# RWKV chunk scan of a hybrid decoder: each chunk's matrices stored as 64 columns on its own half of the partitions

## The chip, the core and the metric

The kernel runs as one program on one core of a Trainium2 chip. The metric is device time in microseconds, from one launch to its end; lower is better. Engines are named as in the profile: PE is TensorE's matmul, PEld its weight load, DVE VectorE, ACT ScalarE, POOL GpSimd, SP SyncE (it issues the DMAs).

## What is computed

One step of a decoder of two layers, for a prompt of 512 tokens and eight decode tokens. Each layer runs three token mixers side by side (retention, differential attention, RWKV-7), merges them by gates, and ends in an MLP. The change touches one stage: the RWKV scan of the prompt, 8 heads of 64 channels, with a 64x64 state per head:

```python
def rwkv7_scan(r, w, k, v, a_vec, b_vec, s0):
    def step(S, inp):
        rt, wt, kt, vt, at, bt = inp
        sa = jnp.einsum('bhij,bhj->bhi', S, at)
        S = S * wt[:, :, None, :] + sa[..., None] * bt[:, :, None, :] + vt[..., None] * kt[:, :, None, :]
        return S, jnp.einsum('bhij,bhj->bhi', S, rt)
    xs = tuple(t.swapaxes(0, 1) for t in (r, w, k, v, a_vec, b_vec))
    S, y = lax.scan(step, s0, xs)
    return y.swapaxes(0, 1), S
...
        yc, s_rwkv = rwkv7_scan(r_h, decay.reshape(hs), k_h, v_h, -kk, kk * a_h, rwkv_s0[l].astype(f32))
```

## The kernel before

A loop on the chip runs the two layers, and a layer is a row of blocks; at the end of a block all engines meet. In a block each engine runs its own list of instructions in the order in which it is written, and waits on semaphores. The scan is one such block (lines 1902 to 2086), and nothing else runs beside it.

The 512 tokens are taken as four blocks of 128 (index `m`), each of two chunks of 64 (index `cc`; `n = 2 * m + cc` counts the chunks). Heads lie in pairs: `hp` is the pair (4), `g` the head in the pair (2), so that a head's 64 channels are one half of the partitions. The token-by-token recurrence of a chunk is replaced by matrices: `products` makes, for each head and block, the 128x128 matrix of inner products of two vectors (four kinds: `m_ba`, `m_br`, `m_ka`, `m_kr`), and DVE's `mask` multiplies it by a triangle mask that is zero outside the two 64x64 diagonal squares, since the two chunks of a block do not mix there. All later products use the 128x128 matrix, zeros and all.

A block `m` has three parts:

- **Lead-in.** DVE makes the start of the inverse (`m1`, then `xt`, lines 2017 and 2018), PE turns `xt` round, ACT copies it to `xm` (L2072), PE makes the `m_ka` products, DVE masks `m_br` and `m_ka` (L2008).
- **Five levels** (`lv` 1 to 5) double the solved part of the triangular system. In each, for `g` = 0 and 1: PE multiplies `m_ba` and `xm` (call it W, bank `pb[g]`), DVE masks the result into `m1` (L2029), PE multiplies `xt` and `m1` (X, `pb[2 + g]`, not at the last level) and `m1` and `xt` (Y, `pb[4 + g]`), and DVE adds X to `xm` (L2042) and Y to `xt` (L2044). In the first level PE also makes the `m_kr` products between W and X.
- **Two chunks**, one after the other. PE: state and `m_ka` times v give the right side, DVE copies it (L2049); `xt` times that gives `uu`, DVE copies it (L2051); then the update of the state in `pb[3]` (`btok` times `uu`, `ktok` times v, as 128x128 of which two squares are wanted), then the output in `pb[2]` (`r_` times the state, `m_br`, `m_kr`). DVE masks the update (L2058), adds it to the state `stb` (L2060) and scales it (L2061), and then the next chunk can start. The `m_ba` and `m_br` products of the next block stand between these on PE.

All operands are fp32. A matmul of this stage shows as two PE records, each with a weight load before it: eight matmuls W of one level are 16 records.

Of the kernel before, what the change touches and what calls it, by code (L numbers as in the profile page):

```python
# [23 lines left out]
P = 128  # L24
# [14 lines left out]
HP = HC // 2  # L39
# [16 lines left out]
for _n, _w in (("ident", P), ("ones", P), ("blk", P), ("inner", HA * P), ("cross", HA * P), ("keep", 2 * P),  # L56
               ("level", 6 * P), ("cosq", 320), ("sinq", 320), ("cosk", 320), ("sink", 320), ("tail", HA),
               ("chunk", HA), ("gamma", HA), ("scan", T), ("c0", HB * DEC), ("c1", HB * DEC), ("selb", DEC),
               ("pair", 2), ("laminit", 2 * DEPTH), ("vmix", DEPTH), ("fold", 9), ("toe", TOE), ("past", NPG * P)):
    COL[_n] = (_c, _w)  # L60
    _c += _w
# [22 lines left out]
def shape_constants():  # L84
# [21 lines left out]
    same = (i[:, None] // CH) == (i[None, :] // CH)  # L106
    before = same & (i[:, None] < i[None, :])
    upto = same & (i[:, None] <= i[None, :])
    put("keep", np.stack([before, upto], 1))
    lv = []  # L110
    for k in range(6):
        m = 1 << k
        lv.append((i[:, None] // (2 * m) == i[None, :] // (2 * m)) & (i[:, None] % (2 * m) >= m)
                  & (i[None, :] % (2 * m) < m))
    lv[0] = lv[0].T
# [88 lines left out]
def build(nc, a, consts, outs):  # L204
# [7 lines left out]
    with ExitStack() as ctx:  # L212
# [257 lines left out]
        with nc.Fori(0, DEPTH) as l:  # L470
# [1422 lines left out]
            m_ba, m_br, m_ka, m_kr = (at(ring[0], n * 1024, 2, HP, P) for n in range(4))  # L1893
            xt = at(arena, 6240, 2, HP, P)
            xm = at(y_raw, 8 * T, 2, HP, P)
            m1 = at(y_raw, 8 * T + 1024, 2, HP, P)
            rhs1 = ring[1][:, 3200:3712]
            uu = arena[:, 7264:7776]
            keep = C("keep", 2, P)
            level = C("level", 6, P)  # L1900
            states_stored = c["stored"].next(256)
            with nc.Block() as block:
                @block.tensor
                def _(pe):
                    def products(left, right, m, bank, g):

                        gs, tok = slice(g * 64, (g + 1) * 64), slice(m * P, (m + 1) * P)
                        for hp in range(HP):
                            t = mm(pb[bank + g][:, hp * P:(hp + 1) * P], left[gs, hp, tok], right[gs, hp, tok])
# [6 lines left out]
                    for m in range(MT):  # L1916

                        for g in range(2):
                            pe.wait_ge(y_added, 12 * m + g + 1)
                            for hp in range(HP):  # L1920
                                t = tr(pb[g][:, hp * P:(hp + 1) * P], xt[:, g, hp, :])
                            t.then_inc(x_made, 1)

                        if m:
                            pe.wait_ge(state_done, 2 * m)
                            pe.wait_ge(out_copied, 2 * m)
                        products(k_, z2, m, 2, 0)
                        products(k_, z2, m, 2, 1).then_inc(ka_made, 1)
                        pe.wait_ge(ba_masked, m + 1)
                        for lv in range(1, 6):  # L1930
                            for g in range(2):
# [4 lines left out]
                                for hp in range(HP):  # L1936
                                    t = mm(pb[g][:, hp * P:(hp + 1) * P], m_ba[:, g, hp, :], xm[:, g, hp, :])
                                t.then_inc(w_made, 1)
                            if lv == 1:
# [4 lines left out]

                                pe.wait_ge(ka_masked, m + 1)
                            for g in range(2):
# [3 lines left out]
                                for hp in range(HP):  # L1950
                                    hs = slice(hp * P, (hp + 1) * P)
                                    if lv < 5:
                                        mm(pb[2 + g][:, hs], xt[:, g, hp, :], m1[:, g, hp, :])
                                    t = mm(pb[4 + g][:, hs], m1[:, g, hp, :], xt[:, g, hp, :])
                                t.then_inc(y_made, 1)
                        pe.wait_ge(kr_masked, m + 1)
                        pe.wait_ge(y_added, 12 * (m + 1))
                        for cc in range(2):
                            n = 2 * m + cc
                            r = slice(cc * 64, (cc + 1) * 64)  # L1960
                            tk = slice(m * P + cc * 64, m * P + (cc + 1) * 64)
                            hsl = [slice(h * 64, (h + 1) * 64) for h in range(HC)]

                            if n:
                                pe.wait_ge(state_done, n)
                            for hp in range(HP):
                                mm(pb[0][r, hp * P:(hp + 1) * P], z2[:, hp, tk], stb[:, hp, :], start=(hp == 0), stop=False)
                            for h in range(HC):
                                t = mm(pb[0][r, hsl[h]], m_ka[r, h % 2, h // 2, r], vtok[r, m, hsl[h]], start=False)
# [4 lines left out]
                            for h in range(HC):  # L1974
                                t = mm(pb[1][r, hsl[h]], xt[r, h % 2, h // 2, r], rhs1[r, hsl[h]])
                            t.then_inc(u_made, 1)
                            if m + 1 < MT:
                                products(z1, (z2, r_)[cc], m + 1, 4 + 2 * cc, 1).then_inc((ba_made, br_made)[cc], 1)
                            pe.wait_ge(u_copied, n + 1)
                            for hp in range(HP):  # L1980
                                hs = slice(hp * P, (hp + 1) * P)
# [3 lines left out]
                            if cc:  # L1985
# [473 lines left out]
```

## Time and profile before

| | us |
|---|---|
| median of 3 runs | 3525.27 (3522.18 to 3531.48) |
| profiled execution, its own time | 3527.91 |
| span of that execution, first to last instruction | 3526.0 |
| the scan, layer 0 and layer 1 | 246.87 and 246.74 |
| one block of 128 tokens in it (`m` = 1, layer 0) | 57.71 |

The span is what the trace shows; 1.9 us of the time lie around it. The scan's two stretches are 493.6 us, 14% of the span. Over the whole span PE is busy 83%, DVE 47%, ACT 22% and POOL 5%. Since each block of the program ends with a meeting of all engines and nothing runs beside the scan, a microsecond that the scan loses or gains is one of the whole.

### The profile page before, as it was taken

The numbers are of one execution on the slowest core, as the hardware profiler recorded it, in microseconds if no ns is written. First come the engines' busy times: TensorE is split into PE (matmuls) and PEld (weight loads), VectorE is DVE, ScalarE is ACT, GpSimd is POOL, SyncE is SP. The second block draws the span as 40 slices with busy tenths as digits, with TensorE's granted clock in tenths as the row PEclk, the third lists the DMA queues.
The fourth block names the chain that finished last, engine by engine and source line by source line (L and its number), as shares of the span: only waits on it lengthen the run. The fifth ranks groups of instructions, "written<-read, shape, count | busy, mean of one in ns | idle before, by whom it ended". The sixth has DMA issues, their size and how long they took to land. (4 is left out here: it accounts for less than half of the span.)

```text
span 3526.0 us, 47932 instructions
## 1 busy us (share of the span) xinstructions
PE 2925.7 (83%) x20182; PEld 2603.1 (74%) x20182; DVE 1643.4 (47%) x2052; ACT 780.9 (22%) x1106; POOL 162.1 (5%) x100
## 2 busy tenths in 40 slices
PE   2698888894899787999948879898849997979898
PEld 1477775793788487999936767578748885979898
DVE  3415345428555564324422441743475546553343
ACT  0221224223100032323302111322320002232331
POOL 0002110200000000000000210121000000000000
PEclk9898998995599688999969889899858986989999
DMA  2413345611000151222241230663100003412221
GB/s 104 179 36 94 101 139 179 206 31 34 13 1 1 42 182 67 77 92 72 72 178 54 57 120 24 226 193 122 47 6 7 1 1 110 157 48 96 72 96 49
DMA packets 212993, 298.61 MB, mean 85 GB/s; under 512 B 27901, under 2 KB 96969, under 8 KB 211492
## 3 DMA queue, kind: packets, MB, share of 16 engines
q1 hardware_dynamic: 212772, 295.47, 25.3%
q8 instruction: 162, 2.65, 0.3%
q14 instruction: 59, 0.48, 0.0%
HBM read 260.30 MB, written 35.14 MB: 84 GB/s over the span
## 5 line engine op out<-in xcount | busy, mean ns | idle before, releaser
L361 PE MATMUL pb<-h_high,f_high 128*128 128x260 f32 x2048 | 417.5, 285 | 62.5 <-ACTq L2319 41.2
L361 PE MATMUL pb<-h_high,f_low 128*128 128x260 f32 x2048 | 416.1, 285 | 0.0
L361 PE MATMUL pb<-h_low,f_high 128*128 128x260 f32 x2048 | 415.1, 284 | 0.0
L361 PEld LDWEIGHTS pb<-h_high,f_high 128*128 128x128 f32 x2048 | 320.2, 191 | 63.7 <-issue 41.9
L511 DVE TENSOR_TENSOR w_low<-ring,w_high 128x2048 fp32r<-128x2048 f32 x64 | 146.7, 2293 | 422.4 <-ACT w_high L503 420.9
L361 PEld LDWEIGHTS pb<-h_low,f_high 128*128 128x128 f32 x2048 | 319.6, 190 | 0.0
L361 PEld LDWEIGHTS pb<-h_high,f_low 128*128 128x128 f32 x2048 | 318.1, 191 | 0.0
L511 DVE TENSOR_TENSOR f_low<-ring,f_high 128x2048 fp32r<-128x2048 f32 x64 | 146.7, 2293 | 349.9 <-ACT h_high L505 204.6
L361 PE MATMUL pb<-w_high,h_high 128*128 128x512 f32 x560 | 225.2, 402 | 52.7 <-ACTq L819 40.8
L738 POOL TENSOR_TENSOR g_low<-yT,g_high 128x512 fp32r<-128x512 f32 x96 | 161.9, 1691 | 2248.3 <-ACT g_high L734 2248.3
L364 PE MATMUL pb<-cst,arena 128*128 128x128 f32 (+5 forms) x566 | 117.0, 351 | 173.5 <-PEq L540 77.8
L361 PE MATMUL pb<-arena 64*128 64x128 f32 (+4 forms) x1520 | 229.7, 349 | 29.6 <-DVE arena L922 9.4
L364 PEld LDWEIGHTS pb<-cst,arena 128*128 128x128 f32 (+5 forms) x566 | 78.1, 170 | 210.3 <-issue 129.1
L361 PEld LDWEIGHTS pb<-arena 64*128 64x128 f32 (+3 forms) x1520 | 184.7, 205 | 63.8 <-issue 38.0
L361 PE MATMUL pb<-w_high,h_low 128*128 128x512 f32 x560 | 224.5, 401 | 0.0
L361 PE MATMUL pb<-w_low,h_high 128*128 128x512 f32 x560 | 224.4, 401 | 0.0
L361 PE MATMUL pb<-h_high,g_high 128*128 128x260 f32 x768 | 169.0, 303 | 45.1 <-POOL g_low L738 24.2
L503 ACT ACTIVATE f_high<-ring 128x2048 fp32r<-128x2048 f32 x64 | 122.6, 1915 | 370.1 <-PE pb L361 342.1
L503 ACT ACTIVATE w_high<-ring 128x2048 fp32r<-128x2048 f32 x64 | 122.1, 1914 | 356.0 <-PE pb L361 219.9
L361 PEld LDWEIGHTS pb<-h_high,g_high 128*128 128x128 f32 x768 | 127.3, 203 | 63.6 <-POOL g_low L738 40.7
L361 PEld LDWEIGHTS pb<-w_high,h_high 128*128 128x128 f32 x560 | 107.5, 192 | 79.3 <-issue 41.6
L361 PE MATMUL pb<-h_low,g_high 128*128 128x260 f32 x768 | 162.2, 294 | 0.0
(309 smaller groups left out, 5287.3 us busy)
## 6 DMA issues: line engine op xcount, KB each, us to landing
ring<-in_w_ff_dram SPq DMA_DIRECT2D x32, 2048.0 KB, 8.5
ring<-in_w_ada_dram SPq DMA_DIRECT2D x20, 2048.0 KB, 8.4
ring<-in_w_in_dram SPq DMA_DIRECT2D x20, 2048.0 KB, 8.7
yT<-in_w_in_dram SPq DMA_DIRECT2D x96, 256.0 KB, 3.6
gate_spill_dram<-yT SPq DMA_DIRECT2D x48, 260.0 KB, 4.2
arena<-gate_spill_dram SPq DMA_DIRECT2D x12, 1040.0 KB, 5.2
arena<-in_w_ada_dram SPq DMA_DIRECT2D x4, 2048.0 KB, 20.4
arena<-in_cache_k_diff_dram SPq DMA_DIRECT2D x32, 256.0 KB, 3.5
```

The source lines that it names most:

```text
L361: return PE.matmul(out, lhsT, rhs, start=start, stop=stop, skip_group_check=True)
L364: return PE.transpose(out, in_, ident[0:in_.shape[0], 0:in_.shape[0]])
L503: t = S.activation(ws[n % 2][0], ring[slot][:, u * 2048:(u + 1) * 2048], ACT.Copy)
L511: t = V.tensor_tensor(ws[n % 2][1], ring[slot][:, u * 2048:(u + 1) * 2048], ws[n % 2][0].bitcast(F32), sub)
L738: G.tensor_tensor(g_split[j % 2][1], g_raw[j % 2], g_split[j % 2][0].bitcast(F32), sub).then_inc(gate_ready, 1)
```

## The change

The two 64x64 squares of a block's matrix are stored below each other instead of on the diagonal of a 128x128 one: chunk 0 on partitions 0 to 63, chunk 1 on partitions 64 to 127, each with 64 columns. So `m_ba` and its like, `xt`, `xm` and `m1` are half as wide, and so are the masks. A product of 128x128 becomes two of 64x64, one for each chunk, from rows and columns 0 to 63 of PE and from rows and columns 64 to 127 in turn (`head_products`). `products` makes the two squares of a head only. The turn of `xt` is no transpose any more but a product with the identity. The state's update is made per head as a 64x64 square on the head's half of the partitions; DVE keeps the state in `stc` in that form, and writes it into the two squares of `stb`, whose other squares stay zero, for the products that read it. In a chunk, products that don't need the state are written ahead of the waits. X and Y share a bank.

```diff
-            m_ba, m_br, m_ka, m_kr = (at(ring[0], n * 1024, 2, HP, P) for n in range(4))
-            xt = at(arena, 6240, 2, HP, P)
+            m_ba, m_br, m_ka, m_kr = (at(ring[0], n * 512, 2, HP, CH) for n in range(4))
+            xt = at(arena, 6240, 2, HP, CH)
...
+            stc, stn = at(ring[0], 2048, HP, DC), at(ring[0], 2304, HP, DC)
+            lower = [slice(cc * CH, (cc + 1) * CH) for cc in range(2)]
...
                         for hp in range(HP):
-                            t = mm(pb[bank + g][:, hp * P:(hp + 1) * P], left[gs, hp, tok], right[gs, hp, tok])
+                            for cc in range(2):
+                                tok = slice(m * P + cc * CH, m * P + (cc + 1) * CH)
+                                t = mm(at(pb[bank + g], 0, HP, CH)[lower[cc], hp], left[gs, hp, tok], right[gs, hp, tok])
                         return t
+                    def head_products(out, left, right, g):
+                        for hp in range(HP):
+                            for cc in range(2):
+                                t = mm(out[lower[cc], hp], left[lower[cc], g, hp], right[lower[cc], g, hp])
                         return t
...
-                                t = tr(pb[g][:, hp * P:(hp + 1) * P], xt[:, g, hp, :])
+                                for cc in range(2):
+                                    t = mm(at(pb[g], 0, HP, CH)[lower[cc], hp], xt[lower[cc], g, hp], ident[lower[cc], lower[cc]])
...
+                            for h, hp, g, hs, gs in heads:
+                                mm(pb[2][r, hs], m_ka[r, g, hp], vtok[r, m, hs], start=(h == 0), stop=False)
                             if n:
                                 pe.wait_ge(state_done, n)
...
+                            upd = at(pb[0], 0, HP, DC)
+                            for h, hp, g, hs, gs in heads:
+                                mm(upd[gs, hp], ktok[r, m, hs], vtok[r, m, hs], start=(hp == 0), stop=False)
...
-                                mm(pb[3][:, hs], btok[r, m, hs], uu[r, hs], stop=False)
-                                t = mm(pb[3][:, hs], ktok[r, m, hs], vtok[r, m, hs], start=False)
+                            for h, hp, g, hs, gs in heads:
+                                t = mm(upd[gs, hp], btok[r, m, hs], uu[r, hs], start=False, stop=True)
                             t.then_inc(update_made, 1)
...
-                            dv(V.tensor_tensor(upd, at(pb[3], 0, HP, P), bc(blk, [P, HP, P], 1), mult))
-                            v.wait_ge(state_read, n + 1)
-                            dv(V.tensor_tensor(stb, stb, upd, add))
-                            V.tensor_tensor(stb, stb, bc(dend[:, :, n], [P, HP, P], 2), mult).then_inc(state_done, 1)
-                            v.wait_ge(state_done, n + 1)
+                            dv(V.tensor_tensor(stn, stc, at(pb[0], 0, HP, DC), add))
+                            for g in range(2):
+                                gs = lower[g]
+                                t = V.tensor_tensor(stb[gs, :, gs], stn[gs], bc(dend[gs, :, n], [DC, HP, DC], 2), mult)
+                            t.then_inc(state_done, 1)
+                            dv(V.tensor_tensor(stc, stn, bc(dend[:, :, n], [P, HP, DC], 2), mult))
```

How the instructions stand, at the three places that the prediction speaks of. A row is a line of the kernel, an operation, what it writes and reads, the size of what it writes (partitions x elements), how many alike follow, and the semaphores that it waits for.

PE, level 2 of a block, the two W and the first X and Y, before (`ring` is `m_ba`, `arena` is `xt`, and `yT` is `xm` or `m1`):

```order
L361 MATMUL pb<-yT,ring 128x128 [waits x_added]
L361 MATMUL pb<-yT,ring 128x128 x3
L361 MATMUL pb<-yT,ring 128x128 [waits x_added]
L361 MATMUL pb<-yT,ring 128x128 x3
L361 MATMUL pb<-yT,arena 128x128 [waits y_added,w_masked]
L361 MATMUL pb<-arena,yT 128x128
```

And in the changed kernel, whose line numbers are one lower here:

```order
L360 MATMUL pb<-yT,ring 64x64 [waits x_added]
L360 MATMUL pb<-yT,ring 64x64 x7
L360 MATMUL pb<-yT,ring 64x64 [waits x_added]
L360 MATMUL pb<-yT,ring 64x64 x7
L360 MATMUL pb<-yT,arena 64x64 [waits y_added,w_masked]
L360 MATMUL pb<-yT,arena 64x64 x7
L360 MATMUL pb<-arena,yT 64x64 x8
```

The order and the waits are the same; each matmul has become two of a quarter of the size, X comes as eight and then Y as eight, where they alternated.

PE, the first chunk of block 0, before (64x128 from `arena` alone are the products with the state, `arena,ring` those with `m_ka`, `m_br` and `m_kr`, `ring,arena` is `xt` times the right side, and 128x128 are `products` and the update):

```order
L361 MATMUL pb<-arena 64x128 [waits y_added,kr_masked]
L361 MATMUL pb<-arena 64x128 x3
L361 MATMUL pb<-arena,ring 64x64 x8
L361 MATMUL pb<-arena 128x128 x4
L361 MATMUL pb<-ring,arena 64x64 [waits rhs_copied]
L361 MATMUL pb<-ring,arena 64x64 x7
L361 MATMUL pb<-arena 128x128 x4
L361 MATMUL pb<-arena 128x128 [waits u_copied]
L361 MATMUL pb<-arena 128x128 x7
L361 MATMUL pb<-arena 64x128 x4
L361 MATMUL pb<-arena,ring 64x64 x16
```

The same chunk in the changed kernel:

```order
L360 MATMUL pb<-arena,ring 64x64 [waits y_added,kr_masked,ka_masked]
L360 MATMUL pb<-arena,ring 64x64 x7
L360 MATMUL pb<-arena 64x128 x4
L360 MATMUL pb<-arena 64x64 x16
L360 MATMUL pb<-ring,arena 64x64 [waits rhs_copied]
L360 MATMUL pb<-ring,arena 64x64 x7
L360 MATMUL pb<-arena 64x64 x8
L360 MATMUL pb<-arena,ring 64x64 x8
L360 MATMUL pb<-arena 64x128 x4
L360 MATMUL pb<-arena 64x64 [waits u_copied]
L360 MATMUL pb<-arena 64x64 x7
L360 MATMUL pb<-arena,ring 64x64 x8
```

The `m_ka` products stand ahead of the state's, half of the update (`ktok` times v) ahead of the first copy, and `m_kr` and `r_` times the state ahead of the second; only half of the update and `m_br` stand behind it.

DVE, the same chunk, before (L2049 and L2051 are the two copies, L2008 masks `m_ba` of the next block, L2058 to L2061 are the state):

```order
L2049 COPY ring<-pb 64x512 [waits rhs_made]
L2051 COPY arena<-pb 64x512 [waits u_made]
L2008 TENSOR_TENSOR ring<-pb,cst 128x512 [waits ba_made]
L2008 TENSOR_TENSOR ring<-pb,cst 128x512
L2058 TENSOR_TENSOR yT<-pb,cst 128x512 [waits update_made]
L2060 TENSOR_TENSOR arena<-arena,yT 128x512 [waits state_read,dve_done]
L2061 TENSOR_TENSOR arena<-arena,small 128x512 [waits dve_done]
```

And in the changed kernel:

```order
L2060 COPY ring<-pb 64x512 [waits rhs_made]
L2062 COPY arena<-pb 64x512 [waits u_made]
L2018 TENSOR_TENSOR ring<-pb,cst 128x256 [waits ba_made]
L2018 TENSOR_TENSOR ring<-pb,cst 128x256
L2069 TENSOR_TENSOR ring<-ring,pb 128x256 [waits update_made,state_read]
L2072 TENSOR_TENSOR arena<-ring,small 64x4x64 [waits dve_done]
L2072 TENSOR_TENSOR arena<-ring,small 64x4x64
L2074 TENSOR_TENSOR ring<-ring,small 128x256
```

The two copies keep their size, the masks are half as wide, and the three steps on the state have become four of half the width, of which three come before the next chunk may read it.

## Rows read from the trace of the kernel before

**Rows 1.** Table by stretch (from:to us, length, busy per engine (records), clock, DMA): the scan, both layers

```profile
943.53:1190.40 246.87, 232.67 (x1956) 215.33 (x1956) 132.12 (x201) 9.51 (x16) 0.00 (x0) 0.88 0.00 1
2669.60:2916.34 246.74, 230.14 (x1958) 212.95 (x1956) 132.15 (x201) 10.27 (x18) 0.00 (x0) 0.89 0.00 1
```

**Rows 2.** Same table: block 1's lead-in, levels, chunks, whole; then block 3, layer 0

```profile
1005.57:1019.39 13.82, 12.12 (x82) 10.95 (x81) 7.84 (x12) 1.79 (x3) 0.00 (x0) 0.75 0.01 1
1019.39:1043.35 23.96, 23.08 (x192) 21.81 (x190) 16.82 (x26) 0.00 (x0) 0.00 (x0) 1.00 0.00 1
1043.35:1063.28 19.93, 19.82 (x220) 18.35 (x220) 8.19 (x13) 0.59 (x1) 0.00 (x0) 1.00 0.01 2
1005.57:1063.28 57.71, 55.02 (x492) 51.11 (x490) 32.85 (x50) 2.38 (x4) 0.00 (x0) 0.94 0.00 1
1121.07:1190.40 69.33, 62.65 (x468) 57.35 (x466) 32.26 (x49) 2.97 (x5) 0.00 (x0) 0.77 0.00 1
```

**Rows 3.** Timeline (start us, length us, instructions xcount, idle before): end of a level, block 0

```profile
968.82 0.39 PE L361 MATMUL pb<-arena,yT 128*128 128x128 f32 x2
969.04 2.10 PE L361 MATMUL pb<-yT,ring 128*128 128x128 f32 x16
969.24 0.69 DVE L2042 TENSOR_TENSOR yT<-yT,pb 128x512 f32<-128x512 f32 x1 [0.50 <-PE pb L361]
969.85 0.68 DVE L2044 TENSOR_TENSOR arena<-arena,pb 128x512 f32<-128x512 f32 x1
970.45 1.43 DVE L2029 TENSOR_TENSOR yT<-pb,cst 128x512 f32<-128x512 f32 x2
971.18 0.30 PEld L361 LDWEIGHTS pb<-yT,arena 128*128 128x128 f32 x2 [0.23 <-DVE yT L2029]
```

**Rows 4.** Timeline: first chunk of block 0 on PE, and DVE's first copy

```profile
985.75 1.06 PE L361 MATMUL pb<-arena 128*64 128x128 f32 x8 [0.87 <-DVE arena L2044]
986.74 1.14 PE L361 MATMUL pb<-arena,ring 64*64 64x64 f32 x16
987.81 1.16 PE L361 MATMUL pb<-arena 64*128 64x128 f32 x8
987.91 0.68 DVE L2049 COPY ring<-pb 64x512 f32<-64x512 f32 x1 [2.32 <-PE pb L361]
989.96 3.91 PE L361 MATMUL pb<-arena 64*128 64x128 f32 x32
993.81 2.08 PE L361 MATMUL pb<-arena,ring 64*64 64x64 f32 x32
995.81 0.43 PE L361 MATMUL pb<-arena 128*64 128x128 f32 x2
```

**Rows 5.** Groups by form (busy us, mean ns, idle): 32-column products; two-column products

```profile
L361 PE MATMUL pb<-arena,xT 128*32 128x512 f32 x32 | 3.6, 595 | 0.6 <-DVEq L1380 0.6
...
L361 PE MATMUL pb<-cst,yT 128*8 128x2 f32 x8 | 0.3, 165 | 0.0
```

**Rows 6.** Timeline: attention scores of one unit; the scan's first products, layer 1

```profile
555.35 1.13 PE L361 MATMUL pb<-arena 64*128 64x512 f32 x4
...
2671.02 2.79 PE L361 MATMUL pb<-arena 64*128 64x128 f32 x32 [1.03 <-PEq L1796]
```

**Rows 7.** Timeline: DVE on 256 elements a partition, in the stage before

```profile
933.80 0.42 DVE L1876 TENSOR_TENSOR ring<-pb,arena 128x256 f32<-128x256 f32 x1 [1.56 <-PE pb L361]
934.14 0.41 DVE L1877 TENSOR_TENSOR ring<-ring,pb 128x256 f32<-128x256 f32 x1
934.58 0.42 DVE L1878 TENSOR_TENSOR ring<-ring,pb 128x256 f32<-128x256 f32 x1
```

**Rows 8.** Table by stretch: second chunk of block 3; start of block 1; 8-row products

```profile
1169.11:1185.79 16.68, 15.04 (x98) 13.66 (x98) 3.46 (x5) 0.59 (x1) 0.00 (x0) 0.50 0.00 0
1008.30:1015.00 6.70, 6.62 (x32) 6.07 (x33) 2.96 (x6) 0.63 (x2) 0.00 (x0) 0.50 0.01 2
...
919.50:933.30 13.80, 13.80 (x62) 12.46 (x61) 8.54 (x22) 1.19 (x2) 0.00 (x0) 0.50 0.11 25
```

More of the change, by code:

```diff
@@ L55 @@
 COL = {}
[L56 to L57 removed]
+for _n, _w in (("ident", P), ("ones", P), ("blk", P), ("inner", HA * P), ("cross", HA * P), ("keep", 2 * CH),
+               ("level", 6 * CH), ("eye", CH), ("cosq", 320), ("sinq", 320), ("cosk", 320), ("sink", 320), ("tail", HA),
                ("chunk", HA), ("gamma", HA), ("scan", T), ("c0", HB * DEC), ("c1", HB * DEC), ("selb", DEC),
@@ L105, in shape_constants @@
     put("gamma", np.broadcast_to(np.exp(log_g)[None], (P, HA)))
[L106 to L109, printed above, removed]
+    row, col = (i % CH)[:, None], np.arange(CH)[None, :]
+    put("keep", np.stack([row < col, row <= col], 1))
+    put("eye", row == col)
     lv = []
@@ L1949, in _ @@
                                     pe.wait_ge(y_added, 12 * m + 2 * (lv - 1) + g + 1)
[L1950 to L1955, printed above, removed]
+                                xy = at(pb[2 + g], 0, 2, HP, CH)
+                                if lv < 5:
+                                    head_products(xy[:, 0], xt, m1, g)
+                                head_products(xy[:, 1], m1, xt, g).then_inc(y_made, 1)
+                        pe.wait_ge(ka_masked, m + 1)
                         pe.wait_ge(kr_masked, m + 1)
@@ L1978, in _ @@
                                 products(z1, (z2, r_)[cc], m + 1, 4 + 2 * cc, 1).then_inc((ba_made, br_made)[cc], 1)
+                            if n:
+                                pe.wait_ge(out_copied, n)
+                            for h, hp, g, hs, gs in heads:
+                                mm(pb[3][r, hs], m_kr[r, g, hp], vtok[r, m, hs], start=(h == 0), stop=False)
+                            for hp in range(HP):
+                                t = mm(pb[3][r, hp * P:(hp + 1) * P], r_[:, hp, tk], stb[:, hp], start=False, stop=False)
@@ L1984, in _ @@
                             t.then_inc(update_made, 1)
-                            if cc:
-                                pe.wait_ge(out_copied, n)
-                            for hp in range(HP):
-                                t = mm(pb[2][r, hp * P:(hp + 1) * P], r_[:, hp, tk], stb[:, hp, :], start=(hp == 0), stop=False)
-                            t.then_inc(state_read, 1)
-                            for h in range(HC):
-                                mm(pb[2][r, hsl[h]], m_br[r, h % 2, h // 2, r], uu[r, hsl[h]], start=False, stop=False)
-                                t = mm(pb[2][r, hsl[h]], m_kr[r, h % 2, h // 2, r], vtok[r, m, hsl[h]], start=False)
+                            for h, hp, g, hs, gs in heads:
+                                t = mm(pb[3][r, hs], m_br[r, g, hp], uu[r, hs], start=False, stop=True)
@@ L1993, in _ @@
                             t.then_inc(out_made, 1)
-                    pe.wait_ge(state_done, 2 * MT)
+                    pe.wait_ge(dve_for_pe, c["pe_from_dve"].next())
                     for hp in range(HP):
-                        t = tr(pb[0][:, hp * P:(hp + 1) * P], stb[:, hp, :])
+                        for g in range(2):
+                            t = mm(at(pb[0], 0, HP, DC)[lower[g], hp], stc[lower[g], hp], ident[lower[g], lower[g]])
                     t.then_inc(pe_for_dve, 1)
@@ L2001, in _ @@
                     dv = c["dve"]
+                    dv(V.memset(stc, 0.0))
                     v.wait_ge(stored, states_stored)
@@ L2024, in _ @@
                         v.wait_ge(ka_made, m + 1)
-                        mask(m_ka, 0, 2).then_inc(ka_masked, 1)
+                        mask(m_ka, 0, 4).then_inc(ka_masked, 1)
                         for lv in range(1, 6):
```

77 lines of the change are left out of this document (36 added, 41 removed).

## The prediction, written before the changed kernel ran

> **What bounds the kernel now.** First the table by stretch: the scan takes 246.87 and 246.74 us [rows 1], together 493.6 of 3526; in it PE is busy 232.67 of 246.87 us, DVE 132.12, and no DMA runs. Only this stage changes, so the question is what each part of one block of 128 tokens waits for. Block 1 takes 57.71 us: 13.82 of lead-in, 23.96 of levels (first add to last), 19.93 of chunks [rows 2]. Four such blocks, a short opening and an end make the layer; block 3 is longer, 69.33 us, because the clock falls to 0.50 (1.2 GHz) in its chunks.
>
> A level repeats every 5.81 us. The timeline shows the loop [rows 3]: the last X and Y record starts 0.11 after 968.82, DVE adds at 969.24 and 969.85 and masks at 970.45, and at 971.18 PE begins the next X and Y. With 32 records of X and Y at 0.11 us (two from 968.82 to 969.04) the loop is 3.52 + 0.31 (from the last record to DVE's start) + 0.61 + 0.60 + 0.73 = 5.77. So it is PE's X and Y plus DVE's two adds and a mask; W (16 x 0.11 = 1.76) lies beside the DVE part. A chunk is PE alone: 985.75 to 995.81, 10.06 us, group after group without a wait worth naming [rows 4].
>
> **The prices that the change needs.** A record of 64x64 after another in the same quarter of PE: 32 take 2.08 us [rows 4], less 0.22 for the last one's length, so 0.060. The change alternates two quarters. What two cost side by side no row shows at 64 columns. The lower bound is full overlap, 0.030 a record; the upper is none, 0.060. I take 0.030, for three rows. Four strips of 32 columns in turn: 32 records of 512 columns in 3.6 us, where one such record alone streams 4 x 0.11 = 0.44, so 14 us in sequence; four ran at once [rows 5]. Two halves of the rows in turn, the attention scores: 4 records in 1.13 us instead of 4 x 0.44 + 0.15 = 1.9 [rows 6]. And in this very stage, at full clock, the 32 opening products of 64 rows, which change the half only every eight records, take 2.79 us instead of 32 x 0.11 + 0.28 = 3.8 [rows 6]. In all three a matmul also stands as two records in sequence before the other strip's come, as it will here. Issue is no limit either: eight two-column records take 0.3 us with 0.165 for the last [rows 5], so at most 0.027 apart. Here the Trainium skill speaks against the change: "TensorE: Matmul & The Clock Gate", section "Wait — 56ns, not 53.3ns?", says that with hardware decode off the sequencer spends about 62 ns on every matmul, which binds once the array's work is shorter. By it nothing would overlap, and the time would be rival 1's; the 0.027 says that this chip doesn't run so.
>
> DVE: 0.42 for 256 elements a partition, 0.34 to the next start where it doesn't depend on the last, 0.44 to 0.46 where it does [rows 7], against 0.61 to 0.73 for 512 [rows 3]. From PE's last record to DVE's start 0.25 (a 64x64 record's 0.22 and 0.03), from DVE's end to PE 0.05.
>
> **Part by part, for one block at full clock.**
>
> *Levels.* X and Y become 64 records: 64 x 0.030 = 1.92. Loop: 1.92 + 0.25 + 0.34 + 0.34 + 0.42 + 0.05 = 3.32. PE's own sum, 96 x 0.030 = 2.88, is below it, so PE no longer binds; DVE's adds and mask do half. From the first add to the end of the last: four loops 13.28, the last Y 2 x 0.48, 0.25 and 0.42, less the first X and Y half and its way to DVE (0.96 + 0.25): 13.7, against 23.96.
>
> *Lead-in.* DVE's first half of `xt` is there after 0.88, its second after 1.68 (was 2.8). From there PE runs the turn of the second half (0.48), `m_ka` (32 records, 0.96), W (0.96), `m_kr` (0.96), and the first X and Y (0.96); with 0.25 to DVE, 6.3 at full clock. ACT's copies (under 0.6 each, [rows 2]) and DVE's masks lie beside these. At 1.2 GHz a pair takes 2 x 0.0534 (half the clock of 64 x 2 columns at 2.4), and 160 records are 8.5; 0.93 + 8.5 + 0.3 = 9.8. Before, the clock stood at 0.50 for 6.7 us in this place of every block [rows 8], after a stretch in which PE waits for DVE; the changed kernel has such a stretch too, only shorter, so I take the middle, 8.1, for blocks 1 to 3, and 9.8 for block 0, which follows a stage at half clock. Before: 13.82.
>
> *Chunks.* On PE, per chunk: two products with the state, each 0.99 with the change of tile size behind it (985.75 to 986.74, [rows 4]); four groups of 16 in one quarter (`m_ka`, `xt`, `m_kr`, `m_br`), 4 x 0.96 = 3.84, and about 0.1 for each of two changes of tile size; and four groups of 16 that alternate between column halves (two of `products`, the two halves of the update), 4 x 0.48 = 1.92. Sum 7.9, against 10.06: what falls away is the update's and the products' empty half. The waits fit beneath: after the state's product PE has 0.96 of work for the 1.04 of the first copy (0.31 + 0.68 + 0.05), more than 2 for the second, and `m_br` and the next `m_ka` (1.92) cover DVE's state steps (0.22 + 0.46 + 0.34 + 0.42 + 0.05 = 1.5). The two copies keep 64x512 and 0.68. In the second chunk the block ends at the update: 7.9 less `m_br` (0.96), 0.25, and 1.65 of DVE until the next lead-in. 7.9 + 6.95 + 0.25 + 1.65 = 16.75, against 19.93.
>
> *Sum.* A block: 8.1 + 13.7 + 16.75 = 38.55, against 57.71. The layer: opening 2.8 (4.5 before, from the first product to the first DVE step); block 0 40.25; blocks 1 and 2 77.1; block 3, whose chunks have no `products` (7.5 and 6.75) and end with the state's steps, a turn by 16 records and a copy (1.6 + 1.2): 38.85. Together 159.0, against 246.8. That the clock holds in block 3's chunks is part of this: they are shorter by the waits and the half-empty update. Twice 87.8 is 175.6. Profiled time 3527.9 - 175.6 = 3352.3; the median lies 2.6 below that execution, so **3350**. Clearing `stc` and the smaller constants cost nothing: DVE waits for the opening products then.
>
> **Rivals.**
>
> 1. *The quarters don't overlap, the clock holds.* A level is bound by PE: 96 x 0.060 = 5.76, no gain on 5.81; levels 23.5, lead-in 10.8, chunks 9.86 + 8.9 + 1.9 = 20.7: a block saves 2.7, block 3 up to 14, the opening 1. Twice about 20 gives 3490. For it: nothing at 64 columns shows an overlap. Against: the three rows above.
>
> 2. *They don't overlap, and the clock doesn't rise.* This is the one that ends slower. PE would stream 64 rows at a time. The rows show that a busy PE isn't enough: with 8-row products it was busy 13.80 of 13.80 us and stayed at 0.50; at the start of block 1, with 64-row products first, 6.62 of 6.70 at 0.50 [rows 8]; and block 3's second chunk took 16.68 instead of 10. At 0.107 a record: lead-in 18.3, levels 4 x 10.3 + 0.4 = 41.5, chunks 17.6 + 15.9 + 1.9 = 35.4, so 95 a block. The layer is longer by 140, the time 3805. It decides from the opening on: block 0 of each layer begins at 0.50, and in this case nothing before the first product with the state would lift it.
>
> 3. *They overlap, but the clock stays at 1.2 GHz throughout.* Level max(96 x 0.0534, 64 x 0.0534 + 1.46) = 5.1; levels 20.9, lead-in 9.8, chunks 28.6: 59.3, 1.6 worse than before in three blocks, but block 3, slow already, gains 10.7 and the opening 1.7. Twice 7.6 gives 3512. For it: each layer's scan opens near the half clock, and in block 3's chunks, which have no `products`, it fell to 0.50. Against: in block 1 it rose once W, X and Y ran, and held 1.00 through the levels and the chunks, whose records are mostly of 64 rows [rows 2].
>
> **How the numbers follow.** Forecast 0.80, rival 1 0.05, rival 3 0.08, rival 2 0.07. About 0.3% (11 us) is what a measurement of this kernel can tell from no change. Forecast and rival 1 are faster, and rival 3 (3512, a gain of 13) in half of its cases: faster 0.89, same 0.04, slower 0.07. Within the forecast: all lead-ins at 6.3 take 11 off, and a level loop without the 0.05s another 10, so 3325; an overlap half good, 0.045 a record, costs 0.96 a level and 8.9 a block, 71 in all, so 3421. The range goes on to rival 1, to 3500: that leaves out rivals 2 and 3 and the forecast's tails, nearly 2 in 10.
>
> **What would show it.** The scan near 159 us a layer. The level loop near 3.3 us, with PE idle between Y and the next X and Y until DVE's mask is done; a row of 32 records of X or Y under 1.2 us. If it is 1.9 and the loop 5.8, the quarters don't overlap. Clock 1.00 through levels and chunks, block 3 no longer than the others; a row of 0.50 across the levels is rival 2 or 3. Chunks 7.9 apart; if more, a wait for `rhs_copied` or `state_done` that I put beneath PE's work. The forecast is wrong if two records in different quarters start 0.06 apart, or if the clock falls where only one quarter streams.

## The result and the profile after

The changed kernel takes 3339.35 us in the median of four runs (3326.39 to 3341.77), the kernel before 3523.72 (3517.59 to 3531.48): a ratio of 0.9478 with a 95% interval of 0.9441 to 0.9515, faster. The forecast was 3350 with a range of 3325 to 3500. The profiled execution is the fastest of the four, 3326.39, with a span of 3324.5; the one before has 3526.0.

The scan's two layers, against 246.87 and 246.74 in [rows 1] and a forecast of 159.0 (table by stretch: from:to us, length, busy time per engine with records, granted clock, DMA share, GB/s):

```profile
941.78:1092.07 150.29, 137.50 (x3344) 127.19 (x3344) 85.86 (x210) 7.79 (x16) 0.00 (x0) 0.97 0.01 3
2563.23:2713.44 150.21, 137.52 (x3344) 127.20 (x3344) 85.85 (x210) 7.79 (x16) 0.00 (x0) 0.97 0.01 3
```

That is 493.6 - 300.5 = 193.1 us less, out of 201.5 between the two spans. The other 8.4 us aren't the change's: the span less both layers is 3032.4 before and 3024.0 after, and over the twelve kernels profiled in this study it lies between 3019.0 and 3035.0 without order. These stages are the same in all of them. So a single execution carries some 8 us either way that the scan has no part in, the two medians of the changed kernel (here and in e0) lie 7 us apart, and small effects are read below from the scan's length, not from the medians.

The parts of block 1, which answer to [rows 2]: lead-in, levels, chunks, whole; then block 0's lead-in, and block 3 of layer 0.

```profile
979.54:986.61 7.07, 6.03 (x171) 5.88 (x173) 4.64 (x13) 0.77 (x2) 0.00 (x0) 0.76 0.01 2
986.61:1000.19 13.58, 12.88 (x381) 11.71 (x375) 9.89 (x26) 0.00 (x0) 0.00 (x0) 1.00 0.01 4
1000.19:1016.79 16.60, 15.47 (x288) 14.32 (x288) 6.79 (x15) 1.18 (x2) 0.00 (x0) 1.00 0.01 3
979.54:1016.79 37.25, 34.38 (x832) 31.91 (x832) 21.32 (x53) 1.95 (x4) 0.00 (x0) 0.95 0.01 3
...
943.70:949.37 5.67, 4.62 (x170) 4.49 (x172) 4.45 (x13) 0.77 (x2) 0.00 (x0) 1.00 0.01 4
...
1054.16:1092.07 37.91, 34.08 (x784) 31.30 (x784) 21.07 (x51) 1.95 (x4) 0.00 (x0) 0.95 0.01 3
```

In block 0's lead-in the 32 records of `m_ka` begin at 945.83 and W behind them at 946.49, those of `m_kr` at 947.42 and X behind them at 948.06 (timeline: start us, length us, engine, line, output<-inputs, shapes, count):

```profile
945.83 0.27 PE L360 MATMUL pb<-arena 64*64 64x64 f32 x1
...
946.49 0.27 PE L360 MATMUL pb<-yT,ring 64*64 64x64 f32 x1
...
947.42 0.27 PE L360 MATMUL pb<-arena 64*64 64x64 f32 x2
...
948.06 0.27 PE L360 MATMUL pb<-yT,arena 64*64 64x64 f32 x1
```

Block 3, 69.33 us before, is no longer an exception: its clock is 0.95. PE's busy time in the scan fell from 232.67 to 137.50 us although its records rose from 1956 to 3344.

A level on DVE, against [rows 3] (timeline: start us, length us, engine, line, output<-inputs, shapes, count, idle before and its releaser). L2053 adds X, L2055 adds Y, once for each half of the heads; L2039 masks W; the PE row is the start of the next X.

```profile
993.15 0.42 DVE L2053 TENSOR_TENSOR yT<-yT,pb 128x256 f32<-128x256 f32 x1 [0.71 <-PE pb L360]
993.49 0.41 DVE L2055 TENSOR_TENSOR arena<-arena,pb 128x256 f32<-128x256 f32 x1
994.08 0.42 DVE L2053 TENSOR_TENSOR yT<-yT,pb 128x256 f32<-128x256 f32 x1 [0.18 <-PE pb L360]
994.42 0.41 DVE L2055 TENSOR_TENSOR arena<-arena,pb 128x256 f32<-128x256 f32 x1
994.75 0.96 DVE L2039 TENSOR_TENSOR yT<-pb,cst 128x256 f32<-128x256 f32 x2
995.22 0.68 PE L360 MATMUL pb<-yT,arena 64*64 64x64 f32 x16
996.42 0.42 DVE L2053 TENSOR_TENSOR yT<-yT,pb 128x256 f32<-128x256 f32 x1 [0.71 <-PE pb L360]
```

The loop, from one L2053 to the next of the same half, is 3.27 us; it was 5.81. The second half's add still waits for PE (0.18), then come an add, an add and a mask (0.42 each, 0.34 from start to start), and 0.05 after the first mask's end PE starts the next X, as in the forecast's sum. On PE, groups of 16 records of one product (timeline):

```profile
955.23 0.63 PE L360 MATMUL pb<-arena,yT 64*64 64x64 f32 x16
955.69 0.63 PE L360 MATMUL pb<-yT,arena 64*64 64x64 f32 x16
```

0.63 from the first start to the last end, less 0.22 for the last record's own length, is 0.41 for seven more pairs: 0.058 a pair, where one quarter alone took 0.060 a record [rows 4]. Two quarters (of 64 rows by 64 columns of PE each) do run side by side.

### The profile page after: what moved, and what is told of

Its sections match the earlier page's. It is cut to its first block and busy times, and to the rows that moved or that the text cites. A ratio compares the mean times of both kernels' runs of the same rounds, so it can differ in the third digit from the quotient of the medians.

```text
span 3324.5 us, 53480 instructions
## 1 busy us (share of the span) xinstructions
PE 2726.0 (82%) x22958; PEld 2423.9 (73%) x22958; DVE 1552.3 (47%) x2070; ACT 777.6 (23%) x1106; POOL 162.9 (5%) x100
## 5 line engine op out<-in xcount | busy, mean ns | idle before, releaser
L363 PE MATMUL pb<-cst,arena 128*128 128x128 f32 (+5 forms) x494 | 95.0, 334 | 158.3 <-PEq L539 78.0
L363 PEld LDWEIGHTS pb<-cst,arena 128*128 128x128 f32 (+5 forms) x494 | 64.8, 163 | 188.9 <-issue 124.2
L360 PE MATMUL pb<-arena 64*64 64x64 f32 (+6 forms) x2288 | 176.7, 279 | 22.3 <-DVE arena L921 9.4
L360 PEld LDWEIGHTS pb<-arena 64*64 64x64 f32 (+4 forms) x2288 | 135.4, 158 | 52.1 <-issue 29.7
```

The costliest lines, as they stand in the source:

```text
L360: return PE.matmul(out, lhsT, rhs, start=start, stop=stop, skip_group_check=True)
L363: return PE.transpose(out, in_, ident[0:in_.shape[0], 0:in_.shape[0]])
```

## Experiments

Each kernel, the profiled spans of both scan layers added up, and the rest of its span. The first four stand against a kernel before of 3522.98 (3517.65 to 3538.44), the next four against 3526.78 (3524.35 to 3533.07), the last two against 3526.67 (3519.79 to 3537.07).

| kernel | median us (range) | ratio to before, 95% | both scan layers | rest of span |
|---|---|---|---|---|
| before | 3523.72 | 1 | 493.6 | 3032.4 |
| changed | 3339.35 (3326.39 to 3341.77) | 0.9478, 0.9441 to 0.9515 | 300.5 | 3024.0 |
| e1 levels, one quarter at a time | 3386.66 (3380.32 to 3393.01) | 0.9608, 0.9521 to 0.9695 | 351.0 | 3027.4 |
| e2 columns in blocks | 3349.16 (3346.57 to 3351.76) | 0.9502, 0.9424 to 0.9579 | 321.6 | 3023.1 |
| e3 DVE doubled | 3378.47 (3370.39 to 3386.54) | 0.9585, 0.9491 to 0.9678 | 349.5 | 3019.0 |
| e4 chunk order of before | 3385.30 (3383.67 to 3386.93) | 0.9604, 0.9527 to 0.9681 | 353.7 | 3028.1 |
| e0 changed kernel again | 3332.27 (3325.34 to 3335.48) | 0.9442, 0.9425 to 0.9458 | 300.7 | 3029.8 |
| e5 levels staggered | 3327.76 (3313.91 to 3333.96) | 0.9443, 0.9427 to 0.9458 | 287.5 | 3024.6 |
| e6 four quarters | 3329.92 (3323.80 to 3332.97) | 0.9435, 0.9420 to 0.9451 | 293.4 | 3035.0 |
| e7 stagger, four quarters, v for both chunks | 3304.51 (3299.14 to 3308.55) | 0.9370, 0.9355 to 0.9386 | 274.4 | 3022.8 |
| e8 early opening | 3308.40 (3304.82 to 3311.64) | 0.9375, 0.9352 to 0.9399 | 279.5 | 3030.3 |
| e9 all, and early opening | 3287.88 (3283.22 to 3290.53) | 0.9317, 0.9293 to 0.9342 | 257.6 | 3029.7 |

**Is it the turn of the quarters? (e1)** In the levels the two chunks' products stand one behind the other instead of in turn; nothing else changes.

```diff
-for hp in range(HP):
-    for cc in range(2):
+for cc in range(2):
+    for hp in range(HP):
         t = mm(out[lower[cc], hp], left[lower[cc], g, hp], right[lower[cc], g, hp])
...
+for cc in range(2):    # X (8 records), then Y (8), of one chunk
```

> The changed kernel with the order inside the level products turned: all of chunk 0 and then all of chunk 1, so that 8 records (W) or 16 (X with Y) in a row use the same quarter of PE. Same work, same waits. Theory A (the gain of the levels is that two quarters of PE stream side by side): most of the overlap goes. With none at all a level is 96 x 0.058 = 5.6 us; where PE looks a few records ahead at each of 8 changes of quarter, as the opening products of before did (1.0 us saved at 3 changes), 4.4 to 4.9. So the loop lies between 4.4 and 5.6 us instead of 3.27, the levels at 18 to 23 instead of 13.6 us a block, and the time at 3390 to 3450 us if the clock holds, up to 3700 if PE falls to 1.2 GHz in the levels. Theory B (the gain is that DVE's masks and adds are half as wide): the loop stays at 3.3 us and the time at 3340.

The loop becomes 4.58 us and the layers 175.4 and 175.6: 50 us for an order alone, so theory B falls. One loop, and PE in it (table by stretch, then timeline):

```profile
955.80:960.38 4.58, 4.58 (x100) 4.50 (x98) 2.26 (x6) 0.00 (x0) 0.00 (x0) 1.00 0.02 4
```

```profile
958.97 0.45 PE L360 MATMUL pb<-arena,yT 64*64 64x64 f32 x5
959.21 0.27 PE L360 MATMUL pb<-yT,arena 64*64 64x64 f32 x1
959.26 0.22 PE L360 MATMUL pb<-arena,yT 64*64 64x64 f32 x1
959.31 0.22 PE L360 MATMUL pb<-yT,arena 64*64 64x64 f32 x1
959.32 0.22 PE L360 MATMUL pb<-arena,yT 64*64 64x64 f32 x1
```

PE is busy throughout: it is the bound again, as in the kernel before. But 4.58 is nearer to the lower end of A's 4.4 to 5.6, and the time just under A's range. The second fence shows why: records go alone, 0.058 apart, until some three are left in their quarter; then the other quarter's first products start between them (959.21, 959.26, 959.31, 959.32). So the overlap doesn't need neighbours in strict turn; it reaches a few records ahead, and where 16 stand in one quarter most of it is lost.

**The same for the other products (e2).** The products that prepare a block (`products`) and both halves of the update run eight records in one quarter before the other's eight; the levels and the turn of `xt` stay as they were.

```diff
-for hp in range(HP):
-    for cc in range(2):        # in products
+for cc in range(2):
+    for hp in range(HP):
...
-for h, hp, g, hs, gs in heads:  # the update, both times
+for h, hp, g, hs, gs in heads[::2] + heads[1::2]:
```

> The changed kernel with the same turn in the products of two vectors and in the two halves of the state's update (same half of the rows, column halves no longer in turn but 8 records of one and 8 of the other). Theory A: these groups of 16 records take 0.75 to 0.95 us instead of 0.48; lead-in 7.1 to about 8.5 us, chunks from 16.6 to 19 or 20 us a block, time about 3365 to 3385 us. Theory C (two column halves of the same rows don't stream side by side anyway, and the chunks gained only by their new order): no change, 3340 us.

The layers take 163.6 and 158.0, 21 us more in all (layer 0 is the longer because its opening and lead-ins met more of a granted clock of 0.50), and the median rises by 10 to 17: between the two theories. The medians alone couldn't tell, since the intervals of the ratios overlap (0.9424 to 0.9579, and 0.9441 to 0.9515). A chunk goes from 7.50 and 7.73 to 8.27 and 8.20, a lead-in at full clock from 5.67 to 6.79; the level loop stays at 3.27. With blocks of eight, the few records ahead are a larger share (timeline, the change from one quarter to the other inside the chunk):

```profile
972.23 0.27 PE L360 MATMUL pb<-ring,arena 64*64 64x64 f32 x1
972.28 0.22 PE L360 MATMUL pb<-arena 64*64 64x64 f32 x1
972.34 0.22 PE L360 MATMUL pb<-ring,arena 64*64 64x64 f32 x1
972.34 0.22 PE L360 MATMUL pb<-arena 64*64 64x64 f32 x1
972.39 0.22 PE L360 MATMUL pb<-ring,arena 64*64 64x64 f32 x1
972.40 0.22 PE L360 MATMUL pb<-arena 64*64 64x64 f32 x1
```

A's price was that of no overlap; the right one is that of an overlap only where quarters meet.

**Does DVE's chain close the loop? (e3)** Before every mask and add of the levels stands one more operation of 256 elements into a tile that nobody reads.

```diff
+V.tensor_tensor(pad[2 + g], bc(level[:, lv], ...), bc(eye, ...), add)
 V.tensor_tensor(xm[:, g], xm[:, g], xy[:, 0], add).then_inc(x_added, 1)
```

> The changed kernel with a second DVE instruction of 128x256, on constants and into a spare tile, ahead of each mask and add of the levels: DVE's part of the levels has its old length again, PE's is untouched. Theory A with the loop of the prediction (X and Y, then two adds and a mask of DVE): 1.87 + 0.25 + 5 x 0.34 + 0.42 + 0.05 = 4.3 us a level instead of 3.27, the levels near 18 us a block, time about 3375 us. If PE alone sets the loop (theory D): 3.3 us and 3340 us.

A loop and the DVE rows in it:

```profile
956.28:960.96 4.68, 3.37 (x104) 3.04 (x101) 4.10 (x13) 0.00 (x0) 0.00 (x0) 1.00 0.02 4
```

```profile
955.94 0.43 DVE L2055 TENSOR_TENSOR ring<-cst 128x256 f32<-128x256 f32 x1 [0.58 <-PE pb L360]
956.28 0.41 DVE L2056 TENSOR_TENSOR yT<-yT,pb 128x256 f32<-128x256 f32 x1
956.62 0.42 DVE L2058 TENSOR_TENSOR ring<-cst 128x256 f32<-128x256 f32 x1
```

The loop is 4.68, 1.41 longer, and 32 loops make 45 of the scan's 49 us: with the doubled steps DVE sets the loop, and theory D's 3.3 falls. That it did so before the doubling isn't shown by this run, since twelve steps of 0.335 are 4.0 us, more than 3.27 whatever bound the loop; e5 below shows it. The size was A's 4.3 plus 0.38, and the first row tells where that comes from: DVE now starts on the first half of X and Y (0.58 of idle there) and has no wait left for the second. Its ten steps up to the first mask, 9 x 0.335 + 0.42, the first half's 0.93 and 0.27, and 0.05 to PE make 4.68. In the changed kernel both halves of X and Y and only three steps stood in this path.

**What the new order in the chunk is worth (e4).** The quarters stay; the products with `vtok`, the update's first part and `r_` times the state go back to where the kernel before has them, behind the waits. The order, in short:

```diff
-m_ka x vtok; wait state_done; z2 x stb; update from ktok
+wait state_done; z2 x stb; m_ka x vtok
...
-m_kr x vtok; r_ x stb; wait u_copied; update from btok; m_br x uu
+wait u_copied; update from ktok, btok; r_ x stb; m_br x uu, m_kr x vtok
```

> The changed kernel with the chunk's products in the order of the kernel before (state before m_ka, the whole update and then r_ times the state, m_br and m_kr behind the second copy), still as quarters. Theory A (a chunk is bound by PE's records, and got shorter because the update and the products lost their empty halves): PE now waits about 0.55 us for each of the two copies, and the chunks go from 16.6 us to about 19 a block; time near 3358 us. Theory E (the new order is what made the chunks shorter): they go back to 19.9 us or more a block, time 3366 us or more.

The layers take 177.4 and 176.4, 53 us more. That is on E's side and beyond A's 3358, but the rows don't show waits of that size. First e4's layer 0, its first chunk of block 0, the second up to the fall of the clock and the rest of it, and most of block 1's second chunk, behind another fall; then the changed kernel's two chunks:

```profile
946.99:1124.36 177.37, 164.25 (x3344) 151.80 (x3344) 85.88 (x210) 7.79 (x16) 0.00 (x0) 0.80 0.01 2
...
969.26:976.85 7.59, 6.65 (x121) 6.00 (x122) 2.45 (x5) 0.00 (x0) 0.00 (x0) 1.00 0.01 2
976.85:983.81 6.96, 6.08 (x117) 5.57 (x117) 2.66 (x5) 0.59 (x1) 0.00 (x0) 1.00 0.01 2
983.81:987.18 3.37, 3.37 (x35) 2.92 (x31) 0.42 (x1) 0.00 (x0) 0.00 (x0) 0.50 0.00 0
...
1019.00:1033.36 14.36, 14.00 (x142) 12.79 (x140) 2.67 (x6) 0.59 (x1) 0.00 (x0) 0.50 0.01 1
```

```profile
1000.19:1007.69 7.50, 7.36 (x142) 6.91 (x143) 2.45 (x5) 0.00 (x0) 0.00 (x0) 1.00 0.01 2
1007.69:1015.42 7.73, 7.73 (x148) 7.16 (x147) 3.08 (x6) 0.59 (x1) 0.00 (x0) 1.00 0.01 4
```

At full clock the old order costs 0.09 us in the first chunk (7.59 against 7.50). The second takes 10.33, of which 3.37 at 0.50; with half of those off it would be some 8.6 (an estimate), against 7.73. That is about 1 us a block, 8 us of the 53. What the old order does besides is to leave PE idle, 0.94 us of 7.59 and 0.88 of 6.96 instead of 0.14 and none, and behind that the granted clock falls to 0.50, where a chunk needs over 14 us. The scan's mean clock is 0.80, not 0.97. So most of the order's worth is the clock it keeps, not the waits that it hides. That the idle time is what brings the clock down here is read from this sequence alone; no run kept the old order without the idle. The kernel before agrees: in its blocks 0 to 2 the chunks leave PE idle for at most 0.15 us and hold 1.00, in block 3 for over 1.6 us each, and there the clock falls.

**The changed kernel again, and what repeats (e0).** An unchanged copy.

> The changed kernel once more, beside the three edits below, to see what repeats. Theory A (quarters overlap in pairs): a scan layer is again 150 us, a level loop 3.27 us, two chunks 16.6 us, and the time is 3326 to 3342. What differs between executions is where the attention stages and the copies ahead of the scan meet a granted clock of 0.5; theory F (the scan itself scatters): the layer differs from 150.3 by more than 2 us.

Layers of 150.36 and 150.35, loops of 3.27, chunks of 7.50 and 7.72: theory A, the scan repeats to 0.1 us, with three falls of the clock in every layer both times. The single lead-ins don't repeat: block 0's is 7.14 here and 5.67 above, block 3's 5.67 here and 7.17 above. Here are two of them, at either clock:

```profile
1055.53:1061.20 5.67, 4.62 (x170) 4.48 (x172) 4.45 (x12) 0.77 (x2) 0.00 (x0) 1.00 0.01 3
1018.16:1025.35 7.19, 6.14 (x171) 6.00 (x173) 4.64 (x12) 0.77 (x2) 0.00 (x0) 0.76 0.01 3
```

It is the same work, 1.5 us apart by whether the clock fell.

**What bounds a level now (e5).** The halves are staggered, so that DVE's steps on one half lie beside PE's products of the other; Y gets banks of its own. In short:

```diff
-for g: W(lv, g);  for g: X(lv, g), Y(lv, g)
+X(lv, 0), Y(lv, 0), X(lv, 1), W(lv + 1, 0), Y(lv, 1), W(lv + 1, 1)
```

> The same products as the changed kernel, but the two halves of heads staggered: X of half 0, Y of half 0, X of half 1, W of half 0 for the next level, Y of half 1, W of half 1; Y goes to banks of its own so that a half waits for its X alone. Theory A: what is left of a level is TensorE work of 6 x 0.47 = 2.8 us plus a wait at the turn of 0.45 us; the stagger covers that wait, a loop is 2.8 to 2.9 us instead of 3.27, 32 loops save some 13 us: 3325 against 3340. Theory G: VectorE's six operations of 0.42 to 0.44 us and their hand-overs set the loop now, it stays at 3.05 to 3.3 and the time falls by 0 to 7 us.

Two loops of e5, and two of the changed kernel:

```profile
956.42:962.02 5.60, 5.60 (x200) 5.60 (x198) 5.08 (x12) 0.00 (x0) 0.00 (x0) 1.00 0.01 3
```

```profile
952.64:959.18 6.54, 6.42 (x199) 5.91 (x196) 4.52 (x13) 0.00 (x0) 0.00 (x0) 1.00 0.02 5
```

A loop takes 2.80, with PE busy for all of it: theory A. So 0.47 of the changed kernel's 3.27 were PE's wait for DVE, and the scan is 13.2 us shorter. The median shows only 4.5 of that against e0; the profiled pair gives 18.4, of which 5.2 lie outside the scan.

**Four quarters (e6).** In `products` both halves of the heads come in turn too. In a chunk this also puts all of `products` ahead of the wait for the first copy, where half of it stood behind.

```diff
 for hp in range(HP):
+    for g_ in range(2):
         for cc in range(2):
```

> The products of 64 columns that open and prepare a block (z1 x z2, z1 x r, k x z2, k x r) take both halves of heads and both chunks in turn, so that four neighbours in the stream lie on all four quarters of the array; written to the same places. Theory H: four quarters run side by side as two do, a pair of records 7 ns apart becomes a group of four, 32 products take 0.47 instead of 0.93 us; four such groups per block lie on the path in part: 10 to 15 us less, 3325 to 3330. Theory I: no more than two products are in flight, whatever their quarters: no change, 3340.

A layer's first 64 records (32 matmuls), in e6 and in the changed kernel (timeline):

```profile
947.85 1.16 PE L360 MATMUL pb<-arena 64*64 64x64 f32 x64 [1.03 <-PEq L1795]
```

```profile
941.78 1.56 PE L360 MATMUL pb<-arena 64*64 64x64 f32 x64 [1.23 <-PEq L1795]
```

1.16 less 0.22 for the last record's length, over 16 groups of four, is 0.059 a group: four run side by side as two do, theory H. The changed kernel's pairs would need 32 x 0.058 + 0.22 = 2.08 there; it takes 1.56, since at its change of half the next records reach ahead. The scan gains 7.1 us, not 10 to 15; the medians can't tell that from nothing (ratio 0.9435 against e0's 0.9442).

**Both, and the products with v for both chunks at once (e7).**

```diff
+if cc == 0:
     for h, hp, g, hs, gs in heads:
-        mm(pb[2][r, hs], m_ka[r, g, hp], vtok[r, m, hs], ...)
+        for rr in lower:
+            mm(pb[2][rr, hs], m_ka[rr, g, hp], vtok[rr, m, hs], ...)
...                              # m_kr into pb[3] likewise
```

> The stagger of the levels and the four quarters together, and in the chunks the products of the masked matrices with v for both chunks side by side (written once per block, 32 products of 64 columns in pairs, in place of 2 x 16 alone). Theory A with H: the stagger saves 13 us, the four quarters 10 to 15, and pairing the products with v 16 x 0.030 us twice per block, about 1 us per block or 8 us if they lie on the path: some 3300 to 3305. If H falls but A stands: 3315 to 3320. If chunks wait on the chain through VectorE rather than on TensorE, the last 8 us are not seen.

The layers take 136.6 and 137.8, 26.3 us less than e0's where the parts of the expectation add up to 31 to 36. The time, 3304.51, lies within the expected 3300 to 3305, but in part by luck: that was counted from 3340, and e0's median is 3332. The second chunk shrinks from 7.73 to 6.21 us; 32 records with v stand in 1.15 us where 16 took 1.11 (timeline, first chunk):

```profile
961.89 1.15 PE L361 MATMUL pb<-arena,ring 64*64 64x64 f32 x32 [0.62 <-DVE arena L2063]
```

**What brings the clock down in the lead-ins (e8).** DVE's opening of the next block moves ahead of its steps on the state, so that the turn of `xt` can follow the last product.

```diff
 V.tensor_copy(uu[r], pb[1][r]).then_inc(u_copied, 1)
+if m + 1 < MT and cc == 1:
+    opening(m + 1)          # m1 and xt, both halves
 v.wait_ge(state_read, n + 1)
...
-mm(at(pb[g], ...), xt[...], ident[...])
+mm(at(pb[2 - g], ...), xt[...], ident[...])
...
+if m and g == 0:
+    pe.wait_ge(state_done, 2 * m)   # ahead of the first W
```

> The changed kernel with one thing moved: the four VectorE operations that open the next block (level 0 of the mask and the identity added, two per half) run in the second chunk, between the copy of U and the wait for the update, and the transposes behind them write to banks that are free by then; the wait for the state moves to the first product that overwrites the update's bank. In the changed kernel TensorE stands idle for 1.93 us between the last product of a block and these transposes, and in most blocks its granted clock is 0.50 for one stretch right behind that. Theory J (the idle brings the clock down): the idle goes, the clock stays at 1.00 through the lead-ins of blocks 1 to 3, and each gains 1.9 + 1.4 us: 6 x 3.0 = 18 us at most, 3315 to 3320. Theory K (the clock falls at a block's start whatever stands before): only the idle is saved, 1.5 to 2 us each, 10 us, 3323 to 3328.

A whole period of 33.21 us, from block 0's chunks into block 1's, and block 1's lead-in, which now begins inside block 0's second chunk, so that its 7.22 us are partly that chunk's:

```profile
978.84:1012.05 33.21, 32.38 (x836) 30.20 (x836) 21.11 (x52) 1.88 (x4) 0.00 (x0) 1.00 0.01 3
```

```profile
984.82:992.04 7.22, 7.22 (x220) 6.98 (x220) 6.13 (x17) 1.29 (x3) 0.00 (x0) 1.00 0.01 2
```

And what stood there in the changed kernel, PE's wait and then the clock:

```profile
980.48 0.33 PE L360 MATMUL pb<-cst,arena 64*64 64x64 f32 x4 [1.92 <-DVE arena L2028]
```

```profile
979.54:981.00 1.46, 0.52 (x16) 0.52 (x16) 1.39 (x4) 0.00 (x0) 0.00 (x0) 1.00 0.00 0
981.00:984.00 3.00, 2.90 (x67) 2.75 (x65) 1.10 (x4) 0.77 (x2) 0.00 (x0) 0.50 0.03 5
```

Theory J: with the idle gone, the clock is 1.00 through every block 1 to 3 of both layers. A block falls from 37.25 to 33.21; PE's idle time by 2.04 (2.87 to 0.83), its busy time by 2.00 (34.38 to 32.38), which is what the half clock had added. I had counted 3.0; over the scan it is 21.2 us against e0 instead of 18, and 3308 instead of 3315 to 3320. The idle is not enough by itself, though: e0's block 3 had the same 1.93 us and kept its clock in both layers, two cases among the twelve lead-ins of blocks 1 to 3 of the changed kernel's two executions. The traces of e1 to e3 and e5 to e7 hold the same wait 36 times more, with a fall at 29 of them. Together that is 39 of 48; without the wait, in e8 and e9, it is none of 12.

**The fastest version (e9).** e7 with the opening of e8.

> The kernel with the staggered levels, the four quarters and the products with v for both chunks side by side, and the early opening on top. Theory J: 3304 less up to 18 us, 3286 to 3290, a scan layer of about 127 us instead of 136. Theory K: 3293 to 3298, a layer of 131.

```profile
942.75:1071.70 128.95, 118.92 (x3344) 111.61 (x3344) 88.78 (x210) 7.59 (x16) 0.00 (x0) 1.00 0.01 3
2547.51:2676.18 128.67, 118.19 (x3344) 111.18 (x3344) 88.78 (x210) 7.60 (x16) 0.00 (x0) 1.00 0.01 4
```

It takes 3287.88 us, theory J's number (the layers are 1.8 us longer than its 127), 1.3% below the changed kernel's second measurement and 6.8% below the kernel before.

## Why the prediction was right, and where its terms were off

- **The price of a pair.** 0.030 a record was chosen over 0.060 from rows of other shapes; measured are 0.029. e1 shows that the turn of the quarters brings it. Rival 1 falls here. The rule of the Trainium skill that stood beside it ("TensorE: Matmul & The Clock Gate", section "Wait — 56ns, not 53.3ns?", 62 ns a matmul with hardware decode off) doesn't bind: at that price e6's first 64 records, which are 32 matmuls, would need 2.0 us, or 4.0 if each record counts as one, and they take 1.16.
- **The level loop.** 3.32 forecast, 3.27 measured; levels 13.7 and 13.58. The rows of a level show DVE's two adds and the mask on the path, e3 that DVE's doubled steps lengthen the loop, and e5 PE's 2.80 beneath, as the sum had it. The sign "PE idle between Y and the next X and Y" is nearly invisible: PE is busy 6.42 of 6.54 us, because each record counts its 0.22 us of length while the pairs start 0.058 apart.
- **Chunks.** 16.75 and 16.60, period 7.9 and 7.73. Right in size, and right that they hold the clock; but the prediction gave the shorter waits no price of their own. By e4 the clock in the chunks hangs on the new order, or on the idle time that it avoids: with the old one the time is 3385, 35 above the forecast.
- **Lead-in: the term that was mis-sized.** 8.1 was the middle between 6.3 at full and 9.8 at half clock. Measured are 5.67 at full clock and 7.07 with a fall inside. The 6.3 took each group of 32 records at 0.96; `m_ka` and `m_kr` change the half of the rows in their middle, where four quarters overlap, and took about 0.65 each, which is the 0.6 by which 6.3 was too long. The rows of block 0's lead-in under the result show it. And only about half of a lead-in runs at half clock, not all of it. Block 0 was put at 9.8 because it follows a stage at half clock; there the clock had risen before it in the profiled execution (5.67), and in e0 it dropped inside (7.14).
- **The sum.** 159.0 forecast, 150.29 measured. Block 0: 40.25 and 35.84 (4.4 of the 8.7); blocks 1 and 2: 77.1 and 74.6 (2.5); block 3: 38.85 and 37.91 (0.9); the opening: 2.8 and 1.92 (0.9). Twice 8.7 is 17.5 more saved than forecast in the profiled pair, but the median fell by 184.4 where 175.6 was forecast: 3339 against 3350. The rest of the difference is the scatter of the other stages, above all that the profiled execution lies 13.0 us below its own median. Against the kernel before of its own round, e0 saves 194.5 us, which is the scan's 193; so the first median shows some 9 us too little, and that 3350 came within 11 us of it is in part luck.
- **Rivals 2 and 3.** The clock was 0.97 over the scan, so neither. What they feared can happen, though: e4 spends long stretches at 0.50 with the same records, and takes 177 us a layer.

## What to carry to other kernels

Small products that use a quarter of the array each cost a fraction when neighbours in the stream lie on different quarters (here 0.029 us a record for two quarters and 0.015 for four, against 0.058 alone), and the order decides: with sixteen records in one quarter the level loop went from 3.27 to 4.58 us. After such a change PE's idle moments are worth more than their length, because the granted clock may fall behind them, as it did at 39 of 48 lead-ins here; look for the 1 to 2 us in which PE waits for another engine's bookkeeping and move that bookkeeping. Read an edit's effect from its stage when the rest of the program scatters by as much.

## What was not expected of the hardware

- The overlap reaches ahead in the stream: with 16 records of one quarter in a row, the next quarter's first products start while some three of the former are still to come (e1).
- Four quarters run at once: 64 records of 64x64 and 64 columns start within 0.94 us, 0.015 each (e6), where one quarter alone needs 0.060.
- Two chunk orders that differ by about 1 us a block at full clock (0.09 measured in the first chunk, the rest estimated) differ by 53 us over the scan's eight blocks, most of it with the granted clock at 0.50 (e4). A wait of 1.92 us of PE was followed by a fall to 0.50 in 39 of 48 lead-ins; without it none of 12 fell (e8, e9). What decided the nine others stays open.
